# Hybrid Hyena / RG-LRU / MLA block on one core: reordered block boundaries, a halved decay table, and modulation products moved beside the first unit

## What is computed

```python
for l in range(DEPTH):                       # DEPTH = 2
    m_lat = adaln(c, ada_w[l], ada_b[l])     # nine vectors: shift, scale, gate for three sub-layers
    m_ctx = adaln(c_ctx[None], ada_w[l], ada_b[l])
    x = half_ffn(x, m[0], m[1], m[2], ...)   # layernorm(ALPHA * x + 0.5 * gate * (silu(a) * u) @ w_out)
    h = modulate(x, m[3], m[4])
    y = even_mixer(h) if l % 2 == 0 else odd_mixer(h)
    x = layernorm(ALPHA * x + m[5] * y)
    x = half_ffn(x, m[6], m[7], m[8], ...)

# in the even mixer, the long convolution's filters:
window = jnp.exp(-t[:, None] * deltas[None, :]) + HY_SHIFT
h = h * window[:, None, :]                   # one window for the forward and the backward filter
k = concatenate([h_fwd, zeros((1, C)), h_bwd[1:][::-1]])   # the backward filter's first row is not used
```

## Time and profile before

| | us |
|---|---|
| median of three runs (lowest, highest) | 2950.17 (2949.54, 2953.34) |
| profiled execution, its own time | 2948.17 |
| its span | 2946.3 |
| mean granted TensorE clock | 0.987 |

### The profile page before, as it was taken

The page is one execution under the profiler, slowest core; times in us unless marked ns, Lnnn a source line. Parts: engine busy times, 40 slices in busy tenths (PEclk is TensorE's granted clock), DMA queues, the critical chain, the costliest instruction groups (busy, mean ns, idle before and its releaser), DMA issues.

```text
span 2946.3 us, 46369 instructions
## 1 busy us (share of the span) xinstructions
PE 2848.6 (97%) x17295; PEld 2471.0 (84%) x17295; DVE 2006.4 (68%) x3254; ACT 1043.4 (35%) x1654; POOL 288.7 (10%) x395
## 2 busy tenths in 40 slices
PE   6999999999999999999999999999999999899998
PEld 2688999987875878898998889999978998878887
DVE  4467767776767467677776787777776886554555
ACT  1422323325650332223223432333265665422223
POOL 1000000001000100101001000000004654000000
PEclk8999999999999999999999999999999999999999
DMA  7444432221213233434431122222310101233331
GB/s 280 149 136 150 134 132 69 64 72 47 60 60 114 86 101 115 158 131 150 145 100 58 43 65 64 78 65 70 88 48 20 29 21 43 58 114 100 100 95 48
DMA packets 301704, 269.78 MB, mean 92 GB/s; under 512 B 31175, under 2 KB 257327, under 8 KB 301456
## 3 DMA queue, kind: packets, MB, share of 16 engines
q1 hardware_dynamic: 278960, 188.95, 21.4%
q0 software_dynamic: 21760, 76.03, 7.3%
q10 hardware_dynamic: 864, 3.15, 0.3%
HBM read 262.85 MB, written 5.24 MB: 91 GB/s over the span
## 4 chain that ended last, share of the span: by engine, by line
PE 88%; DVE 6%; DMA 2%; ACT 1%; issue 1%; SPq 0%; POOL 0%; DVEq 0%; ACTq 0%; POOLq 0%
PE PSALL L2941 14%; PE PSALL L2942 14%; PE PSALL L2943 14%; PE PSALL L3236 8%; PE PSALL L3237 8%; PE PSALL L3238 8%; PE PSALL L3015 2%; PE PSALL L3016 2%; PE PSALL L3017 2%; PE PSALL L2848 2%; PE PSALL L3664 2%; PE PSALL L3649 1%; PE PSALL L2890 1%; DMA RAW<-in_ffn_w_in_dram 1%; PE PSALL L3529 1%
## 5 line engine op out<-in xcount | busy, mean ns | idle before, releaser
L2068 DVE SCALAR_TENSOR_TENSOR X<-PSALL,GATE,X 128x512 f32<-128x512 f32 x480 | 279.9, 612 | 100.0 <-PE PSALL L2943 99.2
L3236 PE MATMUL PSALL<-HHI,WSH 128*128 128x384 f32 x816 | 273.4, 335 | 5.8 <-DVE HLO L2266 5.8
L3237 PE MATMUL PSALL<-HLO,WSH 128*128 128x384 f32 x816 | 273.6, 335 | 0.0
L3238 PE MATMUL PSALL<-HHI,WSL 128*128 128x384 f32 x816 | 272.7, 334 | 0.0
L2941 PE MATMUL PSALL<-GHIA,WHIW 128*128 128x512 f32 (+1 forms) x618 | 217.6, 352 | 13.6 <-DVE X L2068 10.6
L2942 PE MATMUL PSALL<-GLOA,WHIW 128*128 128x512 f32 (+1 forms) x618 | 213.4, 345 | 0.0
L2942 PE MATMUL PSALL<-GLOB,WHIW 128*128 128x512 f32 (+1 forms) x618 | 212.9, 345 | 0.0
L2943 PE MATMUL PSALL<-GHIB,WLOW 128*128 128x512 f32 (+1 forms) x618 | 212.8, 344 | 0.0
L2943 PE MATMUL PSALL<-GHIA,WLOW 128*128 128x512 f32 (+1 forms) x618 | 212.8, 344 | 0.0
L2941 PE MATMUL PSALL<-GHIB,WHIW 128*128 128x512 f32 (+1 forms) x618 | 212.6, 344 | 0.0
L1188 ACT ACTIVATE WSH<-RAW 128x512 fp32r<-128x512 f32 x204 | 129.0, 633 | 222.9 <-DVE RAW L2145 151.2
(11 more groups left out here) (417 smaller groups left out, 7145.8 us busy)
## 6 DMA issues: line engine op xcount, KB each, us to landing
RAW<-in_ffn_w_in_dram SPq DMA_DIRECT2D x176, 512.0 KB, 4.3
ADA<-in_ada_w_dram POOLq DMA_DIRECT2D x144, 512.0 KB, 5.7
RAW<-in_ffn_w_out_dram SPq DMA_DIRECT2D x88, 512.0 KB, 3.7
RAW<-in_ev_w_in_dram SPq DMA_DIRECT2D x20, 512.0 KB, 4.6
WRAW<-in_mla_w_q_up_dram SPq DMA_DIRECT2D x16, 288.0 KB, 3.0
RAW<-in_ev_w_out_dram SPq DMA_DIRECT2D x8, 512.0 KB, 4.3
RAW<-in_mla_w_in_dram SPq DMA_DIRECT2D x8, 512.0 KB, 4.3
RAW<-in_mla_w_out_dram SPq DMA_DIRECT2D x8, 512.0 KB, 4.3
```

What stands on the lines that cost most here:

```text
L2068: dve.scalar_tensor_tensor(X[:, m, lo:lo + n], down_bank(m, s, 2), GATE[:, j, m, s:s + 1], X[:, m, lo:lo + n], ALU.mult, ALU.add).then_inc ...
L3236: te.matmul(out, w_hi, hi[block](k), start=(k == 0), stop=False)
L3237: te.matmul(out, w_hi, low[block](k), start=False, stop=False)
L3238: x = te.matmul(out, w_lo, hi[block](k), start=False, stop=(k == 3))
```

## The change

The window table has one copy; the backward filter's first row is zeroed by a column LATER (1 minus the identity's first column). At the start `ada_products(2)` is moved behind all spectra and beside the first pair, and its gate is formed by DVE after the first residuals. At the boundaries unit B's weights are split earlier, evictions and sums come as their chunks do, centering is woven into the context's lows, and a table BETWEEN places the latents' sums between the steps of `first_pair`. At ffn1 unit B's weights are loaded before unit A's. The diff, cut:

```diff
-    winb = win.copy()
-    winb[0, 0] = winb[LB, 0] = 0.0
-    out["win"] = np.stack([win, winb], 1).transpose(2, 0, 1, 3)
+    out["win"] = win.transpose(1, 0, 2)
...
+    def first_q(name, slot):
+        return plan[name].q + 2 * ((slot == "B") != (name == "ffn1"))
...
+    WIDE_STEPS = (0, 1, (5, 6, 8, 8, 9, 9, 10, 10), 12)
+    BETWEEN = {"ln0": WIDE_STEPS, "ln2": WIDE_STEPS, "ln3": WIDE_STEPS, "ln1": (0, 2, (5, 5, 6, 6, 7, 7, 8, 8), 10),
+               "ln4": (0, 1, (4, 5, 6, 7, 8, 9, 9, 10), 12)}
...
             act.activation(ROOT1[:, 0:1], EPS[:, 0:1], ACT.Sqrt)
+            next_unit(nxt, "B")                        # ACT, end of wide
...
             if name == "ln4":
+                act.activation(ROOT1[:, 0:1], EPS[:, 0:1], ACT.Sqrt)
                 next_unit(nxt, "A")
+            if name == "ln1":
+                next_unit(nxt, "B")
             mean(0)
             for m in range(KC):
                 square(0, m)
+            if name == "ln4":
+                next_unit(nxt, "B", (0,))
+            root(0)
             if name == "ln1":
                 next_unit(nxt, "A")
-                root(0)
-            elif nxt == "mla_in":
-                root(0)
-                next_unit(nxt, "B")
-            else:
-                next_unit(nxt, "B", (0,))
-                root(0)
+            if name == "ln4":
                 next_unit(nxt, "B", (1,))
...
                 for m in range(KC):
-                    if m == 5 and name != "ln1":
+                    if m == 3 and name != "ln1":
                         mean(1)
                     h(0, m)
-                    if m == 5 and name == "ln1":
-                        next_unit(nxt, "B")
...
-        ada_take(2)                                    # ACT, start
         act.wait_ge(tr_taken, plan["ada_first"].tr)
...
-        act.wait_ge(coef_ok, COEF_FIRST)
+        act.wait_ge(coef_ok, COEF_FIRST - 1)
...
         next_unit("ffn0", "B")
+        ada_take(2)
...
+        dve.wait_ge(const_ok, 6)
+        fl(dve.tensor_scalar(LATER[:, 0:1], ID[:, 0:1], -1.0, 1.0, ALU.mult, ALU.add))
...
-        mod_take(2, 2, 2)                              # DVE, start
...
-        def context(name, evict, behind=None):
+        def context(name, evict, first, behind=None):
...
-            early = 0 if name == "ln1" else 2
             for m in range(KC):
+                low(name, 0, m)
                 if m in evict:
                     evict[m]()
-                if m >= KC - early:
-                    center(name, 2, 1, m - KC + early)
-                low(name, 0, m)
                 if m + 3 < KC:
                     norm(name, 2, 0, m + 3)
-            if KC in evict:
-                evict[KC]()
-            for m in range(early, KC):
+                if m >= first:
+                    center(name, 2, 1, m - first)
+            for m in range(KC - first, KC):
                 center(name, 2, 1, m)
...
             for m in range(KC):                        # DVE, end of wide
                 last_chunk(1, m)
+            if nxt == "mla_in":
+                next_unit(nxt, "B")
+            else:
+                next_unit(nxt, "B", (0,))
             last_chunk(0, 0)
+            if nxt != "mla_in":
+                next_unit(nxt, "B", (1,))
...
-            for m in (2, 3, 4):
+            for m in (2, 3, 4, 5):
                 last_chunk(0, m)
...
-            context(then, {0: lambda: last_chunk(0, 5), 1: lambda: last_chunk(0, 6), 2: lambda: last_chunk(0, 7)}, behind)
+            context(then, {0: lambda: last_chunk(0, 7)}, 3, lambda: last_chunk(0, 6))
...
         residual("h0", 2, 0)
+        mod_take(2, 2)
+        dve.wait_ge(mod_ok, ADA_FIRST)
+        gate(0, 0)
+        co_wait()
...
+            next_unit("ffn1", "B")                     # DVE, even_out, after the context's evictions
             out_chunk("ev_out", 2, 1, 0, 4, 5)
             for m in range(KC):
                 center("ln1", 2, 0, m)
             out_chunk("ev_out", 2, 1, 0, 5, 6)
-            next_unit("ffn1", "A")
-            context("ln1", {3: lambda: out_chunk("ev_out", 2, 1, 0, 6, 2), 7: lambda: next_unit("ffn1", "B"),
-                            8: lambda: out_chunk("ev_out", 2, 1, 0, 7, 3)})
+            context("ln1", {1: lambda: next_unit("ffn1", "A", (0,)), 3: lambda: out_chunk("ev_out", 2, 1, 0, 6, 2),
+                            4: lambda: next_unit("ffn1", "A", (1,)), 7: lambda: out_chunk("ev_out", 2, 1, 0, 7, 3)}, KC)
...
-            next_unit("ffn3", "A")                     # DVE, odd_out
             chunk(6, 0)
             chunk(7, 0)
+            next_unit("ffn3", "A")
...
-            context("ln4", {0: lambda: chunk(7, 1)}, lambda: next_unit("ffn3", "B", (1,)))
+            context("ln4", {0: lambda: chunk(7, 1)}, 3, lambda: next_unit("ffn3", "B", (1,)))
...
         spectra(0)                                     # PE, start
         ada_columns(1, 2)
+        for n in range(1, NF):
+            spectra(n)
         ada_products(2, first)
-        spectra(1)
-        ada_products(2, second)
-        spectra(2)
-        ada_columns(2, 2)
-        for n in range(3, NF):
-            spectra(n)
...
+                at_total, at_mean, at_square, at_root = BETWEEN[ln]
+                apart = part(ln, 0)[2] == 0
+                for step in range(2 * KC):
+                    half, k = (step % 2, step // 2) if apart else (step // KC, step % KC)
+                    te.wait_ge(h_lo, h + k + 1)
+                    for slot in "AB":
+                        if half < halves[slot]:
+                            product_step(0, k, slot, half)
+                    if step == at_total:
+                        sums(ln, 2, 1, lambda m: LAST_EVAC[ln], (KC - 1,))
+                    if step == at_mean:
+                        mean_out(ln, 1)
+                    variance(ln, 2, 1, [m for m in range(KC) if at_square[m] == step])
+                    if step == at_root:
+                        root_out(ln, 1)
             for slot in "AB":
                 if ln == "h0":
                     columns(0, [(slot, 0)])
+                    if slot == "B":
+                        ada_columns(2)
                     columns(0, [(slot, 1)])
+                    if slot == "A":
+                        ada_products(2, second)
+                    else:
+                        te.wait_ge(mod_ok, ADA_FIRST)
...
-            sums(then, 2, 1, lambda m: e0 + KC + m + 1)
+            sums(then, 2, 1, lambda m: e0 + KC + m + 1, sum_chunks(then, 1)[:-1])
...
-            ... root_out("ln1", 0) if k == 3 else None)
+            ... root_out("ln1", 0) if k == 1 else None)
```

More of the change, by code:

```diff
@@ L589, in build @@
     WIDE_BANKS = {"ln0": (3, 7), "ln1": (7, 3), "ln2": (3, 7), "ln3": (3, 7), "ln4": (7, 5), "final": (4, 0)}
+    WIDE_STEPS = (0, 1, (5, 6, 8, 8, 9, 9, 10, 10), 12)
+    BETWEEN = {"ln0": WIDE_STEPS, "ln2": WIDE_STEPS, "ln3": WIDE_STEPS, "ln1": (0, 2, (5, 5, 6, 6, 7, 7, 8, 8), 10),
+               "ln4": (0, 1, (4, 5, 6, 7, 8, 9, 9, 10), 12)}
+    LAST_EVAC = {"ln0": last_evac("ffn0", 2, 1, KC - 1), "ln1": plan["ev_out"].evac + 16, "ln2": last_evac("ffn1", 2, 1, KC - 1),
+                 "ln3": last_evac("ffn2", 2, 1, KC - 1), "ln4": plan["mla_out"].evac + 12}
     def adds(name, a):
@@ L2949, in sums @@
             count, done = adds(name, a)
-            for m in [0] + list(range(count + 1, KC)) if ms is None else ms:
+            for m in sum_chunks(name, a) if ms is None else ms:
                 te.wait_ge(*((ln_add, done + count) if m == 0 else (evac, evicted(m))))
@@ L2999, in first_pair, with product_step @@
                            for t in (WHI, WLO)]
-            def columns(a, outs, after=None):
+            def product_step(a, k, slot, half):
                 lo, n, s = part(ln, a)
-                last = {}
+                b, M = 0 if slot == "A" else 3, min(widths[slot], P)
+                if k == 0 and a == 0:
+                    te.wait_ge(lo_done, lo_at[slot] + half + 1)
+                out = PS[b + half][0:M, lo:lo + n] if s == 0 else PS[b + 2][0:M, CTX * half:CTX * half + CTX]
+                hi, low = w[slot][0][:, half, k, :], w[slot][1][:, half, k, :]
+                te.matmul(out, hi, HHI[:, k, lo:lo + n], start=(k == 0), stop=False)
+                te.matmul(out, hi, HLO[:, k, lo:lo + n], start=False, stop=False)
+                return te.matmul(out, low, HHI[:, k, lo:lo + n], start=False, stop=(k == KC - 1))
@@ L3028, in first_pair @@
                     columns(0, [(slot, 0)])
+                    if slot == "B":
+                        ada_columns(2)
                     columns(0, [(slot, 1)])
-                columns(parts_of(ln) - 1, [(slot, half) for half in range(halves[slot])])[slot].then_inc(pe[slot], done[slot])
+                    if slot == "A":
+                        ada_products(2, second)
+                    else:
+                        te.wait_ge(mod_ok, ADA_FIRST)
```

(7 more changed lines are left out.)

69 lines of the change are left out of this document (31 added, 38 removed).

## The result

Before: 2951.76 us, median of 4 runs (a fourth execution, 2955.95, moved it from the 2950.17 given above). Changed: **2919.91 us**, median of 4 (2914.8 to 2922.0). The ratio is 0.9888 with a 95% interval of 0.987 to 0.9906, so 28 to 38 us less. Two repetitions, on two chips, gave 2918.74 (0.9872) and 2919.80 (0.9874). The profiled execution took 2922.01 us, span 2920.0, granted clock 0.991, against 2948.17, 2946.3 and 0.987.

What follows compares the result with a forecast made beforehand. PE's instruction stream plus its waits and slow-clock stretches was taken as the bound. Start 7.4, ln0 and ln2 8.0, ln1 10.5, ln3 1.0, ln4 6.0 sum to 32.9 us off 2948.2; forecast median 2917.0, range 2906 to 2934.

Steps and rivals of the forecast that it cites:

- ln4: Boundary ln4: A's splits move behind evictions, the 2.44 us gap goes, a new 1.9 us wait for a square comes; 6.0 us.
- (a): Start: modulation group 2 moves behind all spectra, so PE's two waits for its loads go; 4.0 us.
- (b): Start: `spectra(1)`, 5.12 us against 3.70 for the same work in `spectra(0)`, regains its clock; 1.4 us.
- Term (c): Start: window table loses half of 3072 KB, so group 0's loads land sooner; 2.0 us, bounds 0 and 4.5.
- Term (d): Start: group 2's second half waits 0 to 1 us for its landing at its new place; taken as 0.
- ln0, ln2: Same boundary twice: sums wait for nothing, root comes 2.85 us earlier, 0.85 of 3.01 us wait remains; 4.0 us each.
- ln1: Boundary ln1: B's splits before centering remove the 3.24 us gap and slow clock, no wait before the latents; 10.5 us.
- ln3: Boundary ln3: `root_out` 0.9 us earlier, with a new 0.9 us wait before it, clock already full; 1.0 us.
- Rival 1: Boundaries: centering, squares and root move as a whole, the 3 us before the latents stay; 2933 us, chance 0.17.
- Rival 2: Four wide boundaries: many short waits hold PE at 1.2 GHz, making the kernel slower; 2997 us, chance 0.03.
- Rival 3: Boundaries: gains hold but the slow-clock stretches stay, 11.4 us; 2928 us, chance 0.07.
- Rival 4: Every boundary: gain lost elsewhere, as DVE's lost cover becomes waits for weights; under 6 us remain, 2948 us, chance 0.03.

Runs made afterwards that it cites:

- u_start: Changed kernel with the start's old order: modulation group 2 between the spectra, its row, bias and gate ahead of the first low; small window table kept; 2923.08 us.
- u_ln1: Changed kernel with ln1's weight splits on ACT and DVE back where they were, PE's places staying new; 2925.96 us (0.9908).
- r_before: The kernel before, run once more without edit for a second trace; 2952.67 us.
- r_same2: The changed kernel without edit, a third time, on the chip of the runs it is compared with; 2919.80 us.
- u_places: Changed kernel with only PE's places of sums, mean and root at the boundaries as before; orders of DVE and ACT stay new; 2934.42 us (0.9934).
- u_center: Changed kernel with DVE's old order of the context's lows and the latents' centering; PE's places and ACT's order stay new; 2925.91 us (0.9901).
- i_steps: Changed kernel with the squares' sums on PE moved and root_out behind step 11 instead of 12 at ln0, ln2, ln3 and ln4; 2921.56 us (0.9888).
- i_both: Changed kernel with the squares' sums and root moved as in i_steps, and modulation group 2's second half behind the latents of A; 2915.70 us (0.9857).
- i_both2: The same kernel as i_both, once more on another chip; 2914.95 us (0.986).

## Why the prediction was right, and where not

The forecast was 2917.0 us (its own terms give 2917.3), in a range of 2906 to 2934; the median came 2.9 us above it. The mechanism held: PE was the bound, the gaps at the boundaries were in good part places in its order, and removing them moved the end. That the total is so near is in part luck: one term of the start failed, a loss in ffn1 was not in the sum, and at ln4 two errors partly cancelled.

- **Start, 7.4 forecast; 6.2 in the mean of traces, 3.0 in the first pair.** Terms (a) and (b) held: both waits for ADA are gone, and `spectra(1)` took 3.60 us. Term (c), the window table's 2.0 us, failed: group 0 landed some 1.2 us earlier, and u_start, with the small table, still ends as before. Term (d), taken as 0, was 0.9 us in the profiled execution and 1.2 in the repetitions, just above its bounds of 0 to 1. The rest was not in the sum: the old order ended the start within 0.2 us in three traces, though the clock from 60 to 68 us was 0.55 to 1.00 in them; the new one passes the clock on, and its start ended between 137.4 and 143.4 us. That the mean comes near 7.4 is in part the chance of the clock.
- **ln0, ln2: 4.0 each; 3.2 and 4.6.** `root_out` was forecast 15 us behind the first step and stood at 15.3; the wait before the latents was forecast 0.85 and was 0.86. The rest is how often the kernel before fell to the low clock: its ln0 took 59.7 and 58.7 us in two traces.
- **ln1: 10.5; 10.3.** No wait at all, 1.00 throughout. The forecast gave all of the first gap to the splits between the lows; u_ln1 shows that the context's root, issued two k earlier, needs those splits moved as much. The prediction did not name that move.
- **ln3: 1.0; 1.7.** In the first pair of traces 0.8. The new wait before the root was 0.57 us (0.9 forecast), and 1.94 us before the latents stayed. The forecast took a full clock for granted there; r_before took 53.0 us.
- **ln4: 6.0; 4.8.** The wait for the square was 1.40 instead of 1.9. Its slow stretch, counted with 1.7 us, was missing in two of three traces and cost 1.35 us in r_same2. Even so `root_out` came 31.9 us behind PE's first sum (2501.91 us) where the forecast has 31.0 (2554.2 against 2523.21 in the trace of before): the first square's sum started at 23.1 instead of 22.1, and from there to the root PE took 8.8 us at the full clock, as much as the forecast counts (8.9) with the slow stretch in it. In the changed kernel's trace a step with a sum behind it took 1.16 us there, where the forecast's price of a step alone is 0.72. So the slow stretch that was counted and did not come stood in for longer steps that were not counted.
- **Between the boundaries, 0 forecast.** ffn1 lost 3.8 us in the mean. In the first pair of traces it lost 3.1, of which 1.9 are one longer wait for a weight load (3.73 instead of 1.84); why the load lands later is open. The cover of DVE, which was the forecast's worry, did not run out: PE waited for no weights behind B's latents at ln0. The one wait for a weight's low part behind a first pair, 1.49 us at ln4, is as long in before.

**The rivals.** Rival 1 (the 3 us before the latents stay, 2933) did not come: 0.86 us are left at ln0 and none at ln1. u_places brings those 3 us back and ends at 2934.42. Rival 2 did not come: at ln0, ln3 and ln4 of the profiled execution waits of 0.3 to 1.9 us left 1.00. The Trainium skill (page "TensorE: Matmul & The Clock Gate", section "A second HAM failure mode: psum-queue depth-cycling") tells of a kernel whose clock swings between the two levels because TensorE often idles very briefly between groups of matmuls. Here this was seen in no whole boundary, only as one slow stretch each behind ln3's 1.94 and ln4's 1.40 us in r_same2, and at the same two places in u_center. Rival 3 fell with the clock rows of the profiled execution; the two stretches in r_same2 cost 2.6 us together. Rival 4 did not come, since the net gain stayed above 27 us.

## What to carry to other kernels

When the busiest engine idles at a seam, list for every step on it when its operand is ready and when it is issued: here moving the sums and the root three to five steps forward, with the other engines' orders new, was worth 13.5 of the 24.6 us that the boundaries gained. A step issued early gains only if the engine that feeds it has nothing in front; the two moves belong together, as u_ln1 shows. A load's wait that looks like a fixed cost may be absorbing scatter from earlier work: removing it gains the wait and makes the time vary. And a gain seen in one stage is not yet a gain of the whole: in i_steps, i_both and i_both2 6.3 us at the boundaries were 2.9 in the spans.

## What was not expected of the hardware

- The same idle time does not always cost the clock. Behind a wait of 3.0 us before the latents, the clock was 1.00 at ln3 in the first trace of before and 0.50 in u_places; at ln0 it was 0.50 in the first trace of before and 1.00 in r_before. Shorter waits cost it in some traces: ln3's 1.94 us was followed by 1.00 in two traces of the changed kernel and by 0.60 in the third. The wait at ln0 in r_before and the clock there:

```profile
694.89 0.50 PE L3015 MATMUL PSALL<-HHI,WHIA 128*128 128x512 f32 x1 [3.01 <-DVE HLO L1842]
```
```profile
694.00:697.00 3.00, 2.11 (x9) 1.00 0.00 0
```

- The boundaries at ln0, ln1 and ln2 repeat within 0.1 us in the three traces of the changed kernel, two of them on different chips, once the long gaps are gone; with the gaps two traces differed by 1.0 to 1.6 us there.
- Loads issued at the same point of a stage land apart: the wait for ffn1's load was 3.73, 4.93 and 4.17 us in three traces of the changed kernel, a scatter as large as several terms of the sum.
